# Layer 0's decay sums spread from rows, four heads in one product, in a two-layer decoder trunk

## What is computed

```python
acs = jnp.cumsum((dt * a).reshape(bsz, nc, q, g, r), axis=2)
diff = acs[:, :, :, None] - acs[:, :, None, :]
lmat = jnp.where(tri, jnp.exp(jnp.where(tri, diff, 0.0)), 0.0)
cb = jnp.einsum('bclgn,bcsgn->bclsg', cc, bc)
y_diag = jnp.einsum('bclsg,bclsgr,bcsgrp->bclgrp', cb, lmat, xdt)
y_off = jnp.einsum('bclgn,bcgrpn,bclgr->bclgrp', cc, h_in, jnp.exp(acs))
```

## Time and profile before

| | us |
|---|---|
| three runs | 1074.95, 1076.21, 1076.57 |
| median | 1076.21 |
| the profiled execution's own time | 1075.52 |
| its span in the profile | 1073.7 |
| PE busy | 1011.5 (94%) |
| DVE busy | 788.8 (73%) |
| ACT busy | 616.2 (57%) |
| mean granted clock of PE | 0.984 of 2.4 GHz |

### The profile page before, as it was taken

The page is one execution under the profiler, slowest core; times in us unless marked ns, Lnnn a source line. Parts: engine busy times, 40 slices in busy tenths (PEclk is TensorE's granted clock), DMA queues, the critical chain, the costliest instruction groups (busy, mean ns, idle before and its releaser), DMA issues.

```text
span 1073.7 us, 26405 instructions
## 1 busy us (share of the span) xinstructions
PE 1011.5 (94%) x9537; PEld 932.0 (87%) x9537; DVE 788.8 (73%) x1645; ACT 616.2 (57%) x1394; POOL 4.9 (0%) x7
## 2 busy tenths in 40 slices
PE   4899979979999999999999999899989999999997
PEld 4899968967799999888999898799877889999886
DVE  1588435468678888977888797765768988888844
ACT  2666636575676666447666675523254476666444
POOL 0000000000000000000000000000000000000000
PEclk8899989999999999999999999999999999999999
DMA  9857663735755665973677552222005856666562
GB/s 347 276 176 247 248 233 120 288 123 158 286 158 181 179 185 181 322 259 110 186 250 226 159 197 79 83 77 81 23 2 180 305 182 177 181 189 177 176 179 95
DMA packets 55835, 195.51 MB, mean 182 GB/s; under 512 B 6179, under 2 KB 8355, under 8 KB 55628
## 3 DMA queue, kind: packets, MB, share of 16 engines
q1 hardware_dynamic: 55756, 194.42, 55.2%
HBM read 193.32 MB, written 1.07 MB: 181 GB/s over the span
## 4 chain that ended last, share of the span: by engine, by line
PE 82%; DVE 9%; DMA 3%; ACT 2%; issue 2%; SPq 1%; DVEq 0%; ACTq 0%
PE proj L554 56%; PE acc L554 25%; DVE w_lo L1640 2%; DMA ada_long<-in_ada_stream 1%; DMA raw<-in_w_stream 1%; SPq L448 1%; DMA ada_ssd<-in_ada_stream 1%; DVE ada_sum L1655 1%; PE acc L813 1%; ACT w_hi L1208 0%; DVE yn L1794 0%; DVE y_mix L2011 0%; DVE x L1801 0%; DVE state L2155 0%; DVE a_lo L2020 0%
## 5 line engine op out<-in xcount | busy, mean ns | idle before, releaser
L1640 DVE TENSOR_TENSOR w_lo<-raw,w_hi 128x512 fp32r<-128x512 f32 x522 | 354.4, 684 | 95.1 <-ACT w_hi L1208 93.1
L1208 ACT ACTIVATE w_hi<-raw 128x512 fp32r<-128x512 f32 x522 | 323.8, 625 | 145.5 <-PE acc L554 117.4
L554 PE MATMUL proj<-h_hi,w_hi 128*128 128x256 f32 x1384 | 395.2, 286 | 3.0 <-DVE conv L1709 1.4
L554 PE MATMUL proj<-h_lo,w_hi 128*128 128x256 f32 x1384 | 393.0, 284 | 1.2 <-DVE h_lo L1845 1.2
L554 PE MATMUL proj<-h_hi,w_lo 128*128 128x256 f32 x1384 | 392.6, 284 | 0.0
L554 PEld LDWEIGHTS proj<-h_hi,w_hi 128*128 128x128 f32 x1384 | 265.4, 192 | 4.1 <-DVE conv L1709 1.8
L554 PEld LDWEIGHTS proj<-h_lo,w_hi 128*128 128x128 f32 x1384 | 265.6, 192 | 1.5 <-DVE h_lo L1845 1.5
L554 PEld LDWEIGHTS proj<-h_hi,w_lo 128*128 128x128 f32 x1384 | 265.3, 192 | 0.0
L554 PE MATMUL acc<-w_hi,a_hi 128*128 128x512 f32 x304 | 123.8, 407 | 4.3 <-DVE w_lo L1640 1.8
L554 PE MATMUL acc<-w_lo,a_hi 128*128 128x512 f32 x304 | 121.4, 399 | 0.0
L554 PE MATMUL acc<-w_hi,a_lo 128*128 128x512 f32 x304 | 121.4, 399 | 0.0
(11 more groups left out here) (307 smaller groups left out, 1276.4 us busy)
## 6 DMA issues: line engine op xcount, KB each, us to landing
raw<-in_w_stream SPq DMA_DIRECT2D x264, 512.0 KB, 3.6
ada_long<-in_ada_stream SPq DMA_DIRECT2D x32, 512.0 KB, 6.8
ada_first<-in_ada_stream SPq DMA_DIRECT2D x24, 512.0 KB, 5.2
ada_ssd<-in_ada_stream SPq DMA_DIRECT2D x16, 512.0 KB, 5.6
ada_out<-in_ada_stream SPq DMA_DIRECT2D x12, 512.0 KB, 4.6
ada_mid<-in_ada_stream SPq DMA_DIRECT2D x8, 512.0 KB, 7.2
ada_ssd<-in_ada_stream SPq DMA_DIRECT2D x8, 256.0 KB, 12.6
bias<-bias_scratch SPq DMA_DIRECT2D x2, 1024.0 KB, 6.1
```

The lines of the kernel that those rows point to most:

```text
L554: return pe.matmul(out, a, b, start=start, stop=stop, skip_group_check=True)
L1208: act.activation(hi, src, ACT.Copy).then_inc(w_rounded, 1)
L1640: dve.tensor_tensor(lo, src, hi.bitcast(F32), ALU.subtract).then_inc(w_split, 1)
```

## The change

The row form of the sums is made once per chunk. Behind the three products of the column sums PE makes four more: 32 columns of `da` as the stationary operand and `triu` as the moving one, to partitions 0 to 31 and again to 32 to 63 of `PB[2]`, for both chunks. A partition then holds one head's running sum as a row of 128 tokens. ACT copies the 64 partitions to `cum_t`, rounded to fp32r (the rounded form, in which a product stands as one record). On partitions 32 to 63 DVE replaces the copy by the difference between the sum and its rounding, so the two halves of `cum_t` are a rounded high part and a rounded low part. DVE then spreads `cum_t` to `cum_rows` with four times as many columns, where a partition's row stands in the quarter of its head's number modulo four and zeros in the others. `decay_rows(n)` becomes one product over 64 partitions and 512 columns, whose stationary operand is a column of `four` (ones at the four heads of the step, in both halves), broadcast to 128 columns.

`decay_rows(0)` and `decay_rows(6)` now also wait for `d_rows`. The semaphores `rel_ones` and `d_masked` go; the masking of `cb` is chained through DVE's own step semaphore. The constants grow by 12 columns. Nothing in the DMA order is moved.

```diff
@@ pe: ssd() @@
                 for b in range(NB):
                     mm(PB[2][:, 24 * b:24 * b + 24], C("triu"), S("da", 24 * b, 24))
-                mm(PB[2][:, 48:72], C("ones"), S("da", 0, 24)).then_inc(d_cum_mm, 1)
+                mm(PB[2][:, 48:72], C("ones"), S("da", 0, 24))
+                for b in range(NB):
+                    for r in (0, 32):
+                        last = mm(PB[2][r:r + 32, P * (b + 1):P * (b + 2)], S("da", 16 * b, 32), C("triu"))
+                last.then_inc(d_cum_mm, 1)
                 project("z0", some=(4,))
...
                     if n >= 2:
                         pe.wait_ge(d_decay, n - 1)
-                    for q in range(4):
-                        col = S("da", 24 * b + h0 + q, 1)
-                        last = mm(AB[n % 2][:, q * P:q * P + P], bc(col, P, P), C("triu"))
-                    last.then_inc(d_decay_mm, 1)
+                    if n in (0, 6):
+                        pe.wait_ge(d_rows, b + 1)
+                    pick = bc(four[0:64, h0 // 4 + 2 * b:h0 // 4 + 2 * b + 1], 64, P)
+                    mm(AB[n % 2][:, :], pick, cum_rows[0:64, b].rearrange("p a b -> p (a b)")).then_inc(d_decay_mm, 1)
@@ act: ssd() @@
                 act.activation(S("tail", 0, 24), S("tail", 0, 24), ACT.Exp).then_inc(d_tail, 1)
+                act.activation(cum_t[0:64].rearrange("p a b -> p (a b)"), PB[2][0:64, P:3 * P], ACT.Copy).then_inc(d_high, 1)
                 stream("z0", copy_z, some=(4,))
@@ dve: ssd() @@
+                dve.wait_ge(d_high, 1)
+                low = cum_t[32:64].rearrange("p a b -> p (a b)")
+                link(dve.tensor_tensor(low, PB[2][32:64, P:3 * P], low.bitcast(F32), ALU.subtract))
+                dve.tensor_copy(four[0:64], C("four", 0, 8, 0, 64))
+                for b in range(NB):
+                    dve.tensor_tensor(cum_rows[0:64, b], bc(cum_t[0:64, b:b + 1].bitcast(F32), 64, 4, P),
+                                      bc(C("mod_four", 0, 4, 0, 64).rearrange("p (a t) -> p a t", t=1), 64, 4, P), ALU.mult).then_inc(d_rows, 1)
                 dve.wait_ge(d_item, 9)
                 stream("z0", some=(4,))
...
                 for b in range(NB):
-                    dve.tensor_tensor(cb[:, b], cb[:, b], bc(one(C("triu")), P, SSD_G, P), ALU.mult).then_inc(d_masked, 1)
+                    link(dve.tensor_tensor(cb[:, b], cb[:, b], bc(one(C("triu")), P, SSD_G, P), ALU.mult))
...
-                    if n in (0, 6):
-                        dve.wait_ge(d_masked, n // 6 + 1)
```

More of the change, by code:

```diff
@@ L79 @@
                   ("keep", 128), ("keep_chunk", 64), ("level", LEVELS * 64),
-                  ("ident_chunk", 64), ("pick", 255)):
+                  ("ident_chunk", 64), ("pick", 255), ("four", 8), ("mod_four", 4)):
     CST[_name] = CST_COLS
@@ L104, in constants @@
     put("ident_chunk", s == t)
+    put("four", p % 32 // 4 == np.arange(8)[None, :])
+    put("mod_four", p % 4 == np.arange(4)[None, :])
     put("pick", np.broadcast_to(np.arange(255) == 127, (P, 255)))
@@ L217, in build @@
         cexp = sb("cexp", [P, 2, 4, P], at=arena + 72 * KB)
+        cum_t = sb("cum_t", [P, NB, P], F32R, at=extra + 1 * KB)
+        cum_rows = sb("cum_rows", [P, NB, 4, P], F32R, at=extra + 2 * KB)
+        four = sb("four", [P, 8], F32R, at=extra + 6 * KB)
         y_ssd = sb("y_ssd", [P, ZT, SEQ], at=at_lo)
@@ L271, in build @@
         act_step, dve_step = sem("act_step"), sem("dve_step")
-        rel_ones, prm_turned, prm_ready, c_ready = (sem(n) for n in ("rel_ones", "prm_turned", "prm_ready", "c_ready"))
+        prm_turned, prm_ready, c_ready = (sem(n) for n in ("prm_turned", "prm_ready", "c_ready"))
         vec_mm, vec_copied = sem("vec_mm"), sem("vec_copied")
@@ L278, in build @@
             sem(n) for n in ("x_sq", "x_part", "x_root", "x_diag", "x_turned", "h_plain", "h_scaled", "h_rounded", "h_ready"))
+        d_high, d_rows = sem("ssd_high"), sem("ssd_rows")
         z_silu = sem("z_silu")
@@ L290, in build @@
         d_stepped = sem("ssd_stepped")
-        d_decay_mm, d_masked, d_diff, d_shifted, d_decay, d_mmat, d_y_mm, d_y = (
-            sem(n) for n in ("ssd_decay_mm", "ssd_masked", "ssd_diff", "ssd_shifted", "ssd_decay", "ssd_mmat", "ssd_y_mm", "ssd_y"))
+        d_decay_mm, d_diff, d_shifted, d_decay, d_mmat, d_y_mm, d_y = (
+            sem(n) for n in ("ssd_decay_mm", "ssd_diff", "ssd_shifted", "ssd_decay", "ssd_mmat", "ssd_y_mm", "ssd_y"))
         d_gated, d_sq, d_sum, d_root, d_inv, d_spread, d_mix, d_rounded, mix_ready = (
@@ L1114, in _ @@
                     pe.wait_ge(in_landed[4], 32)
-                    pe.wait_ge(rel_ones, 1)
                     for v in range(2):
@@ L2252, in mixer @@
                 stream(f"out{layer}", some=range(2 if layer else 6, MIX_T))
-            dve.memset(rel[32:33, :], 1.0).then_inc(rel_ones, 1)
+            dve.memset(rel[32:33, :], 1.0)
             dve.wait_ge(prm_turned, 1)
```

## The result

The changed kernel took 1065.72 us (median of four runs, 1065.33 to 1069.47), the kernel before 1076.39 beside it: a ratio of 0.9911 with a 95% interval of 0.9891 to 0.9931. Two later series of the changed kernel gave 0.9923 (0.9893 to 0.9953) and 0.9908 (0.9883 to 0.9933).

What follows compares the result with a forecast made beforehand. PE was taken to bound the kernel (82% of the chain), with a load loop from quad 9 to 12. 2.06 - 0.07 + 0.11 + 0.30 = 2.40 us took the median 1076.21 to 1073.8; range 1072.2 to 1076.4.

Steps and rivals of the forecast that it cites:

- The constants: Added work: the 12 new columns of constants cost and give nothing, since no row shows a wait on them.
- And take as long as before: Loads between quads 9 and 12: issued sooner by the quad's gain, they take as long as before, 7.4 and 7.5 us.
- the loop: Quads 9 to 12, each waiting for loads into freed slots: six steps' rows, 3.9 us, become waits; gain only 0.11 us.
- forecast waits for quads 10 and 11: Before quads 10 and 11, PE would each time wait about 1.2 us for `ada_ssd`.
- The first three steps: Three steps' decay rows on PE ahead of quad 9: 2.58 + 0.20 - 3 x 0.24 = 2.06 us earlier.
- What is added: New PE products before `d_cum_mm` cost 0.42, of which 0.07 us comes through; the ACT copy and DVE operations delay no one.
- After quad 12: Rows of steps 9 to 11: DVE's 0.30 us wait for PE before the last subtraction goes; gain 0.30, at most 1.95.
- The rival of the clock: PE's wait before quad 12 grows to about 3.9 us and the clock falls, costing up to 3.4; 1076 to 1077.2, chance 0.12.
- The loop does not hold: Quads 9 to 12: loads land sooner or waits are shorter; 1068.4 in full, 1072.5 in part; chance 0.12, 0.02 for full.
- The sum: Whole kernel: 2.06 - 0.07 + 0.11 + 0.30 = 2.40 us gained.

Runs made afterwards that it cites:

- e1: The changed kernel with 12 unused columns of constants left out, so every tensor keeps its old place; 1070.33 us, ratio 0.9944.
- e10: The changed kernel with 56 increments of an unused semaphore at PE's start, moving instruction fetches into open load batches; 1070.67 us, ratio 0.9949.
- e11: The kernel before with 150 increments of an unused semaphore on PE, moving instruction fetches out of the load batches; 1083.44 us, ratio 1.0076.
- e4: The changed kernel run once more, unaltered, for a second trace; 1067.58 us, ratio 0.9923.
- e5: The changed kernel again: its 56 added no-operations were dropped when the program was built; 1066.66 us, ratio 0.9908.
- e14: The kernel before with eleven unused fp32 products filling PE's wait before quad 12; 1074.32 us, ratio 0.9982.
- e13: The changed kernel with ten unused fp32 products of 128 columns filling PE's wait before quad 12; 1067.63 us, ratio 0.9915.
- e6: The kernel before again: its 110 added no-operations were dropped when the program was built; 1075.13 us, ratio 0.9989.
- e2: The kernel before with 12 unused columns more in the constants, giving tensors behind them the changed kernel's places; 1071.47 us, ratio 0.9966.
- e3: The kernel before with an empty 32 bytes ahead of `a_hi` and everything behind it moved; 1071.96 us, ratio 0.9959.
- e7: The kernel before with every SBUF tile, `w_hi` and `h_hi` too, moved 32 bytes further; 1073.69 us.
- e8: The kernel before with `a_hi` and `a_lo` alone moved by 32 bytes within the 64-byte period, everything behind by 64; 1074.29 us.
- e9: The kernel before with every tile moved 32 bytes, and `a_hi`, `a_lo` and all behind another 32; 1072.17 us.

## Why the prediction was wrong

**The constants** failed most. The sentence "the 12 columns of constants cost and give nothing" took them for a matter of waits. They move `a_hi` and `a_lo` by 32 bytes onto the same half of 64 bytes as the weights, and 912 products become 5.4 ns shorter: 4.9 us by the rows, 3.7 and 4.4 by the ratios with only the layout changed (0.9966, 0.9959), 2.3 to 3.9 between e1 and the changed kernel. No rival held this, and it is why the time came out below even the lowest of them, 1068.4. But it isn't all: e1, the change without the new places, took 1070.33, and that too is below 1072.2. Here already held the number that mattered, 0.24; nothing in one trace could say that it depends on an address. The Trainium skill, page "TensorE: Matmul & The Clock Gate", section "Back-to-back issue gap", was weighed there with about 131 ns; the rows of both layouts, 227 and 233 ns, stay far above it.

**"And take as long as before"**, of the loads, is the step that failed in the loop. The 7.4 and 7.5 of the earlier trace rows were each the time of a load in a batch with an instruction fetch in it; without one the last load lands 6.1 to 6.5 behind its issue. With a fetch in every batch the loop was near its limit, as the prediction says: e10, with the new product and the fetches, shows a wait of 0.61 before quad 10. Without them it isn't. PE's own pace sets it in the kernel before, where quads 10 and 11 have no idle time ahead of them, and in the changed kernel too; I took a landing that came 0.35 before its use for a bound that would stay. With fewer instructions in a step the fetches of the changed kernel come later against the batches and mostly miss them, a by-product that the prediction did not weigh. So quads 9 to 12 start 10.16, 10.16 and 9.8 apart where the forecast had about 11 each. Of the forecast waits for quads 10 and 11 one was seen, 1.24, in the one execution whose second batch took 9.22.

The two effects can be parted with four kernels. From D to quad 12, with the fetches in the batches: 42.2 (median of the kernel before and its layouts), changed 39.03 (e10). With the fetches out: 40.80 (e11), changed 37.3 (e1, e4, e5). The product is worth 3.2 to 3.5 us, the fetches 1.4 to 1.7, together 4.9; e10 and e11 are one trace each. That agrees with the rows: 1.40 up to quad 9 and two pairs of steps at 0.93 are 3.26. The forecast for the same stretch was 2.06 + 0.11 = 2.17; the 0.07 for the added work lies ahead of D.

**The first three steps** gave 1.40 in place of 2.06. The mis-sized term is the new product, 0.43 alone and 0.63 for two, where 0.24 was taken from a stream of such products. In such a stream the next weight load starts with the product before it, as two rows of the changed kernel's output projection show. Behind the lone product of 176.82 it starts 0.43 later, at 177.25, together with its own product, and the gap behind that stays:

```profile
262.35 0.19 PEld L560 LDWEIGHTS acc<-w_hi,a_lo 128*128 128x128 f32 x1
262.35 0.39 PE L560 MATMUL acc<-w_hi,a_hi 128*128 128x512 f32 x1
```

```profile
177.25 0.19 PEld L560 LDWEIGHTS proj<-h_hi,w_hi 128*128 128x128 f32 x1 [0.24 <-issue]
```

The two rows of products take 1.06 in place of 2.58, which is 1.52; 0.12 of it is lost in the units of z, which take 3.06 each from their first product to what follows, where they took 2.96 and 3.04. In the loop a step saves 0.93 / 2 = 0.47, not 0.65.

**What is added** was right in what comes through: from the first column sum to the first decay row it takes 7.80 to 7.82 us in place of 7.70, so 0.10 to 0.12 is lost where 0.07 was forecast. The price was low: by the start of what follows, the eight records hold PE for 0.56, not 0.42, and only PE's idle time before the states covered it. ACT's copy cost nothing, and DVE's four operations took 1.81 us, with `cum_rows` ready 1.8 us before its use.

**After quad 12** the wait went as forecast, and what it is worth stays open. The wait of 0.30 of the earlier trace rows is gone in the row that answers to it, from e4's timeline of DVE:

```profile
222.21 1.12 DVE L1972 TENSOR_SCALAR lmat<-acc,small 128x128 f32<-128x128 f32 x4
```

Before and after can be compared at the full clock in e14 and e13: from quad 12 to the outputs of step 10 it takes 11.12 and 10.58, so 0.54 is gained there. From there on e13 ran at the lower clock, and at the output projection 0.05 is left (14.74 and 14.69).

**The rival of the clock** was built on a wait of 3.9 before quad 12, which didn't come: the wait is 2.49 to 2.70 in the changed kernel (after, e1, e4, e5). The clock fell all the same, in these four executions and in e10. But it also fell in the kernel before: in e6, which is the same program, and in e2, e3, e7, e8 and e9, which differ from it in places alone. The one execution that I read, with its wait of 2.64 and a clock of 1.00, was the exception. The fall costs about the same in both kernels, 16.3 against 14.7 us from quad 12 to the output projection, so 1.6 where the rival had up to 3.4; as far as these traces tell, it makes no difference between them. It goes with PE's idle time: with 2.49 to 3.54 us of it ahead of quad 12 the clock fell in 11 of 12 executions, with 1.76, 1.52, 0.49 and 0.30 in none, and filling the wait (e13, e14) kept it up. Further on in the stage it also fell at shorter waits, at one of 1.75 in e13. The falls at quad 12 agree with the section "Why this matters for your kernels" of the same page of the Trainium skill, which warns of idle gaps between bursts.

**"The loop does not hold"** was the rival that came nearest, at 1068.4 or 1072.5. It had loads that "land sooner" as its reason, which is what happened in the loop. It was given 0.12, and e1's 1070.33 lies between its two values. That the whole kernel went lower still was luck: the place of two tiles, which no one had chosen.

**The sum** as measured: 4.9 up to quad 12 for the product and the fetches together, less 0.1 for what is added, 0.05 to 0.5 behind quad 12, and 2.3 to 4.9 for the place. That is 7.2 to 10.2, against 8.3 to 9.9 by the three series' ratios. Without the place it is 4.9 to 5.3, and e1 measured 6.0 (3.8 to 8.4).

## What to carry to other kernels

Before a small change is credited or blamed, look at what it moves without meaning to: the address of every tile behind a grown one, and the instruction count of the engine that fetches most. Both can be tested in a run each, by a hole of 32 bytes and by a few instructions without work at the start. A landing that comes just before its use is no bound as long as the engine shows no idle time there; whether it becomes one depends on how long the next load takes. A load's duration read from one execution includes what else fell into it. A clock that holds or falls in one execution must be looked up in a second one before a rival is built on it.

## What the runs showed of the hardware

- Rounded products of 128x128 by 512 columns start 227 to 228 ns apart when the stationary and the moving tile begin on the same half of 64 bytes, 233.4 when on different halves; all four combinations of the two halves were run. Products of 256 columns stood at 120.0 in all runs, with their two tiles on the same half in each.
- A fetch of 16 KB of instructions within the first 6.6 us of an open batch of four 512 KB loads lengthens it from 7.4 to 7.8 us to 8.1 to 9.5; where it falls into SP's issuing, one issue takes 0.7 to 2.1 us in place of 0.43.
- A lone rounded product of 512 columns over 64 partitions, with a column broadcast as the stationary operand, holds PE for 0.42 to 0.43 us.
- Increments of a semaphore on PE follow each other 0.15 us apart: 56 of them at the start put its first product at 9.52 us, where it stands at 4.24 to 4.37 without them.
